# Down projection of a two-layer encoder step: weight sums moved from VectorE to GpSimd, high parts also copied to PSUM

## The reference

```
h = rmsnorm(x, p['norm_ffn_pre'][i])
f = jnp.square(jax.nn.relu(h @ p['w_up'][i])) @ p['w_down'][i]
x = x + rmsnorm(f, p['norm_ffn_post'][i])
```

## Time and profile before

| | |
|---|---|
| Median of 3 runs | 1782.18 us (1780.83 to 1782.9) |
| Profiled execution, its own time | 1780.53 us |
| Its span in the trace | 1778.7 us |
| PE busy | 1684.8 us, 95% |
| DVE busy | 1155.3 us, 65% |
| ACT busy | 836.0 us, 47% |
| POOL busy | 579.0 us, 33% |
| Granted clock, mean | 0.991 |

### The profile page before, as it was taken

One profiled execution on the slowest core, in us unless ns is written; L12 is line 12 of the kernel. 1 busy time (PEld: TensorE's weight loads), 2 busy tenths in 40 slices (PEclk: granted clock), 3 DMA queues, 4 the chain that ended last, 5 costly groups with the idle time before them and its releaser, 6 DMA issues. The chain is left out here.

```text
span 1778.7 us, 31700 instructions
## 1 busy us (share of the span) xinstructions
PE 1684.8 (95%) x12611; PEld 1609.3 (90%) x12611; DVE 1155.3 (65%) x2100; ACT 836.0 (47%) x1606; POOL 579.0 (33%) x361
## 2 busy tenths in 40 slices
PE   6999999999999999999999999989999999999996
PEld 5987877998999999998899999987998899999996
DVE  6437777315774838477879797957306774838477
ACT  6426666324433434345455666555424534434342
POOL 1231211241443343432135344440341353343431
PEclk9999999999999999999999999999999999999998
DMA  6621121121322312221223222331221222313221
GB/s 224 210 72 58 58 66 31 60 84 48 106 84 72 105 64 105 72 102 54 76 81 106 91 95 90 107 102 56 72 84 43 100 84 80 111 60 107 70 97 54
DMA packets 51491, 153.11 MB, mean 86 GB/s; under 512 B 12400, under 2 KB 14160, under 8 KB 51088
## 3 DMA queue, kind: packets, MB, share of 16 engines
q1 hardware_dynamic: 43968, 139.99, 22.9%
q10 hardware_dynamic: 7376, 11.10, 2.0%
HBM read 144.16 MB, written 6.47 MB: 85 GB/s over the span
## 5 line engine op out<-in xcount | busy, mean ns | idle before, releaser
L1189 PE MATMUL ps<-big_hi,w_hi 128*128 128x288 f32 x2528 | 559.4, 301 | 12.0 <-POOL w_lo L2411 4.7
L1189 PE MATMUL ps<-big_lo,w_hi 128*128 128x288 f32 x2528 | 540.1, 297 | 7.4 <-DVE big_lo L1665 7.2
L1189 PE MATMUL ps<-big_hi,w_lo 128*128 128x288 f32 x2528 | 544.5, 295 | 0.0
L2411 POOL TENSOR_TENSOR w_lo<-raw,w_hi 128x1024 fp32r<-128x1024 f32 x116 | 283.5, 2445 | 682.3 <-ACT w_hi L611 572.9
L1189 PEld LDWEIGHTS ps<-big_hi,w_hi 128*128 128x128 f32 x2528 | 408.8, 189 | 20.8 <-issue 13.1
L1189 PEld LDWEIGHTS ps<-big_lo,w_hi 128*128 128x128 f32 x2528 | 402.1, 189 | 12.7 <-DVE big_lo L1665 11.8
L1189 PEld LDWEIGHTS ps<-big_hi,w_lo 128*128 128x128 f32 x2528 | 407.8, 189 | 0.1
L1479 PE MATMUL ps<-col_hi,w_hi 128*128 128x288 f32 x896 | 267.6, 299 | 19.0 <-DVE mix L2058 18.3
L1479 PE MATMUL ps<-col_hi,e_lo 128*128 128x288 f32 x896 | 264.4, 295 | 0.0
L1479 PE MATMUL ps<-col_lo,w_hi 128*128 128x288 f32 x896 | 264.1, 295 | 0.0
L611 ACT ACTIVATE w_hi<-raw 128x1024 fp32r<-128x1024 f32 x176 | 185.7, 1055 | 153.6 <-DMA raw<-in_slabs 88.7
(11 more groups left out here) (223 smaller groups left out, 2285.7 us busy)
## 6 DMA issues: line engine op xcount, KB each, us to landing
raw<-in_slabs SPq DMA_DIRECT2D x238, 512.0 KB, 3.3
row<-acs_prompt ACTq DMA_DIRECT2D x16, 384.0 KB, 4.0
bias<-in_alibi SPq DMA_DIRECT2D x12, 256.0 KB, 2.7
x<-in_x SPq DMA_DIRECT2D x2, 1152.0 KB, 8.5
out_h<-state ACTq DMA_DIRECT2D x4, 384.0 KB, 2.6
out_y<-x SPq DMA_DIRECT2D x2, 576.0 KB, 2.8
raw<-in_slabs SPq DMA_DIRECT2D x4, 256.0 KB, 3.8
kms<-in_mk SPq DMA_DIRECT2D x2, 512.0 KB, 5.2
```

The costliest lines, as they stand in the source:

```text
L1189: ins = pe.matmul(ps[:, bank + h, 0:hi_c - lo_c], weight(w, s, kt), a[:, k0 + kt, lo_c:hi_c], start=start, stop=stop, skip_group_check=True)
L2411: pool.tensor_tensor(w_lo[:, s % RING], raw[:, s % RING], w_hi[:, hi_place(s)].bitcast(F32), ALU.subtract).then_inc(lo_done, 1)
```

## The change

Four things change, all in the down stage.

1. `weight_sum` moves from DVE to POOL. Within pairs 0 to 2 of a chunk POOL works in the order entries 0, 1, 2, 4, 5, 3, 6, in pair 3 in the order 0 to 6. In pair 0 it waits with entry 6 until all low parts of the columns are made.
2. ACT, behind the high part of each S entry, copies this high part once more, to PSUM (two banks in turn). It waits for its own high part, and for the low part made two S entries earlier (`s_lo_done`).
3. DVE makes the low parts of S entries from the sum in SBUF and the copy in PSUM, at other places of its order.
4. In the up stage ACT takes entry 3 one tile later, and PE waits for the last low part of the last pair before it writes a norm sum to the same bank.

```diff
+        def s_copy(layer, c, p, k):
+            return ps[:, S_COPY_BANK + sums_before(c, p, k) % 2].rearrange("p (j c) -> p j c", j=PAIRS_DOWN)
...
+                    if kind[0] == "S":
+                        nth = 4 * pair_number(layer, c, p) + sums_before(c, p, k)
+                        act.wait_ge(*hi_of_entry(layer, c, p, k))
+                        if nth > 1:
+                            act.wait_ge(s_lo_done, nth - 1)
+                        act.activation(s_copy(layer, c, p, k), e_hi[:, place].bitcast(F32), ACT.Copy).then_inc(s_copied, 1)
...
-                            for e in (1, 2, 3):
+                            for e in (1, 2):
                                 entry_hi(c, e)
                         else:
-                            for e in (4, 5):
+                            for e in (3, 4, 5):
                                 entry_hi(c, e)
...
+                    pe.wait_ge(s_lo_done, 4 * pair_number(layer, c, p) + 4)
                     half_sum(0)
...
-                def weight_lo(c, p, s):
-
-                    k, place = place_of(c, p, s)
-                    dve.wait_ge(*hi_of_entry(layer, c, p, k))
+                def weight_lo(c, p, nth):
+                    k = [k for k, kind in enumerate(products(c, p)) if kind[0] == "S"][nth - 1]
+                    s, place = products(c, p)[k][1], fifo_place(layer, c, ENTRIES * p + k)
+                    dve.wait_ge(s_copied, 4 * pair_number(layer, c, p) + nth)
                     read_by = {True: {3: 2, 2: 4, 1: 3, 4: 4}, False: {1: 2, 2: 4, 3: 3, 4: 4}}[is_last(c, p)][s]
                     dve.wait_ge(s_summed, 4 * pair_number(layer, c, p) + read_by)
-                    dve.tensor_tensor(e_lo[:, place], e_raw[:, place], e_hi[:, place].bitcast(F32),
+                    dve.tensor_tensor(e_lo[:, place], e_raw[:, place], s_copy(layer, c, p, k),
                                       ALU.subtract).then_inc(s_lo_done, 1)
...
                         add_to(mix_half[:, c11 + 1], ps[:, f, 0:HALF]).then_inc(freed, 1)
...
+                        if p == 0:
+                            weight_lo(c, 1, 1)
+                        elif p == 1:
+                            weight_lo(c, 2, 2)
+                        elif ahead and not turned:
+                            weight_lo(c, 3, 2)
+                            weight_lo(c, 3, 3)
                         end(6)
                         add_to(mix_half[:, c11 + 2], ps[:, a, 0:HALF]).then_inc(freed, 1)
-                        if ahead:
-                            weight_lo(c, p + 1, 4)
+                        if turned:
+                            weight_lo(c, 3, 2)
+                            weight_lo(c, 3, 3)
+                            weight_lo(c, 3, 4)
+                        elif p == 2:
+                            weight_lo(c, 3, 4)
...
+                    pool.wait_ge(*place_free(layer, c, ENTRIES * p + k))
+                    if sums_before(c, p, k):
+                        pool.wait_ge(s_summed, 4 * number + sums_before(c, p, k))
...
-                        for k in range(ENTRIES):
-                            if products(c, p)[k][0] == "A":
-                                entry_lo(c, p, k)
+                        for k in (range(ENTRIES) if p == PAIRS_DOWN - 1 else (0, 1, 2, 4, 5, 3, 6)):
+                            if p == 0 and k == ENTRIES - 1:
+                                pool.wait_ge(col_lo_done, 4 * PAIRS_DOWN * (FF_CHUNKS * layer + c + 1))
+                            entry_lo(c, p, k)
```

More of the change, by code:

```diff
@@ L2103, in down @@
                         add_to(mix_half[:, c11], ps[:, a, 0:HALF]).then_inc(read_done, 1)
+                        if p == 1:
+                            weight_lo(c, 1, 3)
+                        elif p == 2:
+                            weight_lo(c, 2, 4)
                         if p == 0:
@@ L2108, in down @@
                             columns_lo(c, 3, 6, 7)
-                            end(2)
+                        end(2)
+                        if p == 0:
                             dve.wait_ge(freed, g0 + 2 * p)
-                            add_to(mix_half[:, c11 + 1:c11 + 4:2], ps[:, a:f + 1:step, 0:HALF]).then_inc(read_done, 1)
-                            weight_lo(c, 0, 4)
-                        if ahead and not turned:
-                            weight_sum(c, p + 1, 1)
-                            weight_sum(c, p + 1, 2)
-                            if p:
-                                weight_lo(c, p + 1, 1)
-                        if p:
-                            end(2)
-                            add_to(mix_half[:, c11 + 1:c11 + 4:2], ps[:, a:f + 1:step, 0:HALF]).then_inc(read_done, 1)
-                        if ahead and p:
-                            weight_sum(c, p + 1, 3)
-                        if turned:
-                            weight_sum(c, p + 1, 2)
-                            weight_lo(c, p + 1, 3)
+                        add_to(mix_half[:, c11 + 1:c11 + 4:2], ps[:, a:f + 1:step, 0:HALF]).then_inc(read_done, 1)
+                        if p in (0, 1):
+                            weight_lo(c, p, 4)
+                        elif ahead and not turned:
+                            weight_lo(c, 3, 1)
                         if c == FF_CHUNKS - 1 and p:
@@ L2440, in ffn, with place_of, weight_sum @@
             def ffn(layer):
+                def place_of(c, p, s):
+                    k = products(c, p).index(("S", s))
+                    return k, fifo_place(layer, c, ENTRIES * p + k)
+                def weight_sum(c, p, s):
+                    number, first = pair_number(layer, c, p), pair_slab(layer, c, p)
+                    k, place = place_of(c, p, s)
+                    a11, a12, a21, a22 = [a_block(layer, c, p, ("A", i, j)) for i in range(2) for j in range(2)]
+                    for t in (first, first + 1):
+                        pool.wait_ge(raw_in[t % RING], 16 * (t // RING + 1))
+                    pool.wait_ge(*place_free(layer, c, ENTRIES * p + k))
+                    if sums_before(c, p, k):
+                        pool.wait_ge(s_summed, 4 * number + sums_before(c, p, k))
+                    part = lambda i: e_raw[:, place_of(c, p, i)[1]]
+                    if s == 3:
+                        ins = pool.tensor_tensor(part(3), a11, a21, ALU.subtract)
+                    elif s == 4:
+                        ins = pool.tensor_tensor(part(4), a12, part(2), ALU.subtract)
+                    elif is_last(c, p):
+                        if s == 2:
+                            ins = pool.tensor_tensor(part(2), a22, part(3), ALU.subtract)
+                        else:
+                            ins = pool.tensor_tensor(part(1), part(2), a11, ALU.add)
+                    elif s == 1:
+                        ins = pool.tensor_tensor(part(1), a21, a22, ALU.add)
+                    else:
+                        ins = pool.tensor_tensor(part(2), part(1), a11, ALU.subtract)
+                    ins.then_inc(s_summed, 1)
                 def entry_lo(c, p, k):
                     kind, place = products(c, p)[k], fifo_place(layer, c, ENTRIES * p + k)
+                    if kind[0] == "S":
+                        weight_sum(c, p, kind[1])
+                        return
                     pool.wait_ge(*hi_of_entry(layer, c, p, k))
```

40 lines of the change are left out of this document (15 added, 25 removed).

## The result

| | before | after |
|---|---|---|
| Median | 1782.1 us (1780.83 to 1782.9, 4 runs) | 1803.1 us (1801.32 to 1803.68, 4 runs) |
| Ratio to before, 95% interval | | 1.0118 [1.0105, 1.013] |
| Span of the profiled execution | 1778.7 us | 1799.1 us |
| Granted clock, mean | 0.991 | 0.985 |

The forecast was slower, 1789.5 us, with a range to 1806. The direction held and the time lies in the range, but the kernel loses 21 us instead of 7.4.

What follows compares the result with a forecast made beforehand. PE, busy 95%, was taken to bound the kernel, so only its waits count. Its down-stage losses of 5.7 + 3.0 + 3.0 + 6.2 = 17.9 us a layer against 14.2 gave +7.4 in all: 1789.5 us, range 1777 to 1806.

Steps and rivals of the forecast that it cites:

- T: Zero of the forecast's hand-made timeline of a down stage in a chunk like 1; a product takes 1.6 us, a pair 11.2.
- "cancel": Rival for the whole kernel: gains and stalls cancel, giving 1779 to 1785.7 us; chance 14%.
- the first: Rival: POOL has S4 of pair 3 by about T+35.3, its 2.35 us wait goes, kernel faster at 1776.8 us; chance 24%.
- the fourth: Rival: DVE's low parts with a PSUM input still exclude POOL, some 20 us more a layer, 1829 us; chance 5%.
- +3.7 a layer: Down stages: PE's forecast losses of 17.9 us a layer against 14.2 worked out for the old order; +7.4 in all.
- list was compared with list: Summing step: new order's hand-made 17.9 us a layer set against the old order's hand-made 14.2, not the trace's 13.1.
- "Pair 2 is the same, 10.0 later": POOL's chain in a chunk like 1: pair 2's instructions follow pair 1's times, each 10.0 us later.
- The list of the old order: Hand-made sum of PE's down-stage losses before the change: 14.2 us a layer where the trace has 13.1.
- "How firm": Sensitivity to POOL's instruction time: 0.01 us on one is 1.7 us on the kernel; 1.19 gives -8, 1.535 gives +48.
- "POOL keeps ahead": Rival: POOL's 10.0 us of work a pair stays ahead of PE's 11.2, so the kernel gets faster, 1776.8 us; chance 24%.
- The third rival: A POOL sum takes 1.35 to 1.5 us, with stalls of 0.3 to 1.4 in pairs 1 and 2: 1801 to 1827; chance 15%.

Runs made afterwards that it cites:

- e2: Changed kernel, but POOL makes its entries in the order 0, 1, 2, 4, 5, 3, 6 in pair 3 of chunks 0 to 2 too; 1788.3 us, ratio 1.0022.
- e3: Changed kernel, but in chunk 3 ACT makes the two squares of pair 0's tiles ahead of pair 2's entries; 1803.6 us, ratio 1.0112.
- e4: Changed kernel without ACT's copies: sums stay on POOL, DVE makes the low parts from two SBUF operands; 1813.2 us, ratio 1.0164.
- e1: Changed kernel with extra PE matmuls, results overwritten, put into its long waits in the down stages; 1800.5 us, ratio 1.0093.

## Why the prediction was right in direction and wrong in size

**What held.** The sums that stand inside a down stage cost 1.29 us (mean 1.294, longest 1.311), the copy 0.60, the freed low part 0.68. The 32 sums of pair 0 are made ahead of the stage, and 16 of those took 1.40 to 1.70, which lifts the mean of all 128 to 1.33. S4 of pair 1 was due at T+13.9, and a row of it in chunk 1 (start 601.07, 1.30 long) ends at T+13.91, with T now 588.46. That is in part luck: the chain began 0.2 us early (S1 ended at T+9.5, not 9.7), and from one sum to the next it took 1.46 where I had 1.4. The two large new waits came where they were put and at their sizes: 2.3 against 2.35 at product 2 of pair 3, 3.9 against 3.85 at product 6 of pair 1 in chunk 3. The first is shown to be POOL's order (e2), the second the squares (e3). The rival "cancel", the first and the fourth are out. In particular the PSUM input does free the low part, which e4 puts at some 10 us.

**What failed is the sum.** It gave +3.7 a layer. The stages show +8.4 in layer 1 and +11.4 in layer 2, 12.4 us more in all. Three steps failed: the clock behind a wait was put at nothing, list was compared with list and not with the trace, and "Pair 2 is the same, 10.0 later" was too short. In the prediction's own measure (from a stage's first matmul to the next stage's, in chunk 3 to the norm sum, less its matmuls at 0.1333 us) the 12.4 us are:

- 3.0 us, the clock in chunks 1 and 2 of layer 2, shown by e1. A wait was costed at its own length. Behind a wait of 2.13 us PE got 1.2 GHz for 3.4 us in those two stages, and with nothing late behind it that cost 1.5 us each time. No term stood for it.
- 2.2 us, the step "I compare list with list". The list of the old order was 1.1 us a layer above its trace, and I took that for an error that both lists share. Against the trace the same working gives +4.8 a layer. The list of the new order was not above its trace but below, 17.9 against 21.5 in layer 1 and 24.5 in layer 2.
- 3.1 us, chunks 1 and 2 without the clock: they lose 4.0, 3.7, 3.7 and 3.7 us where I had 3.0 each. This is the pace of POOL's chain. I had pair 2's sums 10.0 us behind pair 1's. They came 10.66 later, as POOL's and then ACT's rows of chunk 1 below show: A22's low part waits 1.21 us for ACT, and ACT's copy of S4 had itself waited 0.49 for a low part of DVE's. By the starts of its products PE lost 0.54 where I had 0.2 (product 2 of pair 1), and 0.37 where I had nothing (product 6 of pair 2). This part is read from rows; no run isolates it.
- 4.1 us, chunks 0 and 3: they lose 6.8 and 7.1 us in layer 1, 6.8 and 7.3 in layer 2, where I had 5.7 and 6.2. In chunk 0 the clock has no part, as e3's trace shows; there, at the full clock, the same small waits in pairs 1 and 2 make most of the excess. In chunk 3 the length stayed with the clock at 1.00 (e1). The extra matmuls could have cost there what the clock gave back; the new wait of 0.99 us speaks for the first reading, and what makes chunk 3's last microsecond stays open.

```profile
594.17 2.55 POOL L2459 TENSOR_TENSOR e_lo<-raw,w_hi 128x512 fp32r<-128x512 f32 x2 [5.39 <-DVE col_lo L2012]
596.68 1.29 POOL L2446 TENSOR_TENSOR e_raw<-raw 128x512 f32<-128x512 f32 x1
...
604.82 2.55 POOL L2459 TENSOR_TENSOR e_lo<-raw,w_hi 128x512 fp32r<-128x512 f32 x2 [1.21 <-ACT w_hi L901]
607.34 1.28 POOL L2446 TENSOR_TENSOR e_raw<-raw 128x512 f32<-128x512 f32 x1
...
603.53 0.60 ACT L911 ACTIVATE ps<-w_hi 128x512 f32<-128x512 f32 x1 [0.49 <-DVE e_lo L2036]
```

One step of "How firm" does not follow. At 1.7 us for each 0.01 a sum of 1.19 us gives -15 and one of 1.535 gives +43, not -8 and +48.

**The rivals.** "POOL keeps ahead" failed by its condition, since S4 of pair 3 ended at T+37.9 and not T+35.3. One edit of POOL's order (e2) made the condition true, S4 then ending at T+34.9, and the wait went. But chunks 1 and 2 then gained 1.0 to 1.2 us on the kernel before and not 1.9, and with chunk 3's loss the kernel stayed slower. The third rival needed a POOL sum of 1.33 us or more. In the stage it took 1.29, but POOL's slower pace through its waits for ACT brought what that rival named, small waits in pairs 1 and 2, and with the clock also its time.

## What to carry to other kernels

Work moved to an engine with spare time is worth what its slowest chain allows, not what the averages say: look for an instruction of the new owner that waits for a third engine ahead of one that others need, and put it behind. Here that was the difference between 1803 and 1788 us. Cost a long wait of PE (here 1.9 to 3.8 us) with the slow stretch that can follow it, and check whether something later in the stage is late anyway: in chunk 0 the slow stretch then cost nothing. And compare a hand-made list with the trace itself, not with a second list, when it misses the trace in a known case.

## What the runs showed that was not expected

- The same wait of 2.13 us was followed by the full clock in layer 1 and by half of it in layer 2, and in e3's trace by the full clock in chunk 1 of layer 2. A wait of that length may or may not cost the clock.
- With the slow stretches of the down stages gone (e1), chunks 0 and 3 (52 and 53.5 us) kept their length.
- The two halves of the change do not add: sums alone +1.6%, copies alone 0.0%, together +1.2%.
- ACT took 602 ns to copy 128x512 from SBUF to PSUM, where it took about 628 ns (L901) from SBUF to SBUF, and the shortest and the longest of the 128 copies were 601 and 604 ns. The Trainium skill, "ScalarE: Activation LUTs", section "Step-by-step: what each stage is for", says that ScalarE writes PSUM faster than SBUF. The trace agrees, by 4%, though the SBUF row also rounds to fp32r.
